# Stick-breaking sums as two rounded fp32r products instead of one f32 product

## Chip, core and metric

The kernel runs on one core of one Trainium2 chip. The metric is the device time of one execution in microseconds (us), as the median of several executions. The profile shown is of one more execution, taken by the hardware profiler.

## What is computed

Two blocks of a network, one after the other, on 512 tokens of width 1024. The change lies in the stick-breaking attention of the second block, which has 8 heads of width 128:

```
z = einsum('bhqd,bhkd->bhqk', q, k) * scale
causal = s_idx < t_idx
log_1mb = where(causal, log_sigmoid(-z), 0.0)
suffix = cumsum(log_1mb, axis=3, reverse=True) - log_1mb
log_a = log_sigmoid(z) + suffix
a = where(causal, exp(log_a), 0.0)
out = einsum('bhqk,bhkd->bhqd', a, v)
```

For a key s, `suffix` is the sum of the log terms of all later keys. In the kernel the keys lie on the 128 partitions, so that sum is a matrix product: with a triangle of ones inside a block of 128 keys, with a full matrix of ones over later blocks.

## The kernel before

All of the model is one program, written out by hand for each engine, with semaphores between them. The scores of a head are causal, so key block kb (0 to 3) only meets the query columns from 128*kb on: 512, 384, 256 and 128 columns. The four pieces of a head stand side by side in one tile of 1280 columns, at the offsets `offs` = 0, 512, 896, 1152. Three "parts" are worked on at a time, in the order m = 2, 1, 0: part 2 holds key blocks 2 and 3 (384 columns), part 1 key block 1 (384), part 0 key block 0 (512).

For each head h, in a pipeline over rounds:

- TensorE (PE), `sb_scores`: z of the head, an f32 product of 512, 384, 256 or 128 columns for each key block, to PSUM banks 4 to 6 (line L664).
- ScalarE (ACT): Abs (L970), Exp (L972), Ln (L974) of z, giving log(1+exp(-|z|)) in `sbt`; then, for the head before, the Exp that gives the weights a (L982), and the rounded copy `oH` of the output of two heads back (L977).
- VectorE (DVE), once the Ln is done (`sb_t`): for each part, `Lp` = max(z,0)+t, the negated log(1-beta) (L1170), then log beta in `sbt` (L1171), then the causal mask of the diagonal block (L1174, L1176). The last of these sends `sb_L`. I call these ten instructions the block of a head.
- PE, `sb_sums`: for each key block one f32 product of `Lp` with the triangle `low` (L672), and one with `ones` for every later key block (L675), summed in banks 0 to 2. In all ten f32 products a head: one of 512 columns, two of 384, three of 256, four of 128.
- DVE: subtracts the sums from log beta (L1190); ACT takes the Exp, DVE masks it (L1184), PE multiplies by v (L706), DVE takes the rest `oL` of the output (L1161).

PE's program is a fixed list. Round h holds, for kb = 3, 2, 1, 0 in turn, the scores of head h+1 and the sums of head h; then the product with v of head h-1; then `GATE_BLOCKS[h]` pieces of other work, (8, 8, 8, 5, 4, 4, 3, 4, 4) for the rounds 0 to 8. Such a piece is one eighth of a weight tile of the gate projection: three fp32r products of 512 columns (L1513 to L1515). After the rounds follow the tiles of `branch_sb` (operand `sb_oH`). The waits in the two functions are

```
E.at("sb_L", 3 * h - min(kb, 2))      # sb_scores(h, kb)
E.at("sb_L", 3 * h + 3 - min(kb, 2))  # sb_sums(h, kb)
```

so neither the scores of head h+1 nor the sums of head h start before the first `sb_L` of head h; key block 1 wants the second and key block 0 the third.

GpSimd (POOL) makes of every f32 weight tile in `sb_raw` a rounded part `wH` (L1496) and a rest `wL` (L1501). It has room for two rests, so each L1501 waits for PE to finish a tile. When a gate tile is complete, ACT copies it from bank 7 to `merged` (L1819) at places set by `GATE_COPIES = {0: 1, 1: 2, 2: 3, 3: 4, 5: 5, 7: 6, 9: 7}` (round of ACT: tile); the next gate tile uses the same bank and waits for that copy. Tile 5 is complete after the third gate piece of PE's round 4, and tile 6 with the last piece of round 6.

Of the kernel before, what the change touches and what calls it, by code (L numbers as in the profile page):

```python
# [19 lines left out]
P = 128  # L20
F32 = mybir.dt.float32
F32R = mybir.dt.float32r
# [7 lines left out]
S = 512  # L30
# [156 lines left out]
def build(nc, a, first=True, second=True):  # L187

    with ExitStack() as ctx:
# [7 lines left out]
        def sb(name, shape, dt=F32, on=None):  # L197
            return (on or ctx).enter_context(nc.sbuf_tensor("sb_" + name, shape, dt))
# [5 lines left out]
        par = sb("params", [P, N_KEPT])  # L204
        xT = sb("xT", [P, KB, S])
        hH = sb("hH", [P, KB, S], F32R)
# [14 lines left out]
        def C(name, i=0, n=None):  # L221
            o, w = CONSTS[name]
            return cst[:, o + i:o + i + (n or w)]
# [362 lines left out]
        def sb_in(first, kb):  # L586

            at = P * 2 if kb == TB - 1 else 0
            return ps[first + min(kb, 2)][:, at:at + qw[kb]]
# [3 lines left out]
                 (0, slice(offs[0], offs[1]), slice(0, qw[0]))]  # L593
        sb_t = [B["sbt"][:, c, :] for c in range(2)]
        V_BANK = (6, 2, 0, 1)
        sb_a = [b[:].rearrange("p s t -> p (s t)")[:, 0:1280] for b in (sq, tmp)]
# [15 lines left out]
        def second_pe(E, products, products_and_sums, parts_ready, one_tile, part_of_tile, rows_tile, turn, h_hi, h_lo):  # L612
# [56 lines left out]
            def sb_sums(h, kb):  # L669
                E.at("sb_L", 3 * h + 3 - min(kb, 2))  # L670
                E.at("sb_la", 3 * h - min(kb, 2))
                mm = nc.tensor.matmul(sb_in(0, kb), C("low"), B["Lp"][:, offs[kb]:offs[kb] + qw[kb]],  # L672
                                      start=True, stop=True)
                for later in range(kb + 1, TB):
                    mm = nc.tensor.matmul(sb_in(0, kb)[:, P * (later - kb):], ones,  # L675
                                          B["Lp"][:, offs[later]:offs[later] + qw[later]],
                                          start=False, stop=True, skip_group_check=True)
                if kb < TB - 1:
                    mm.then_inc(sems("sb_S"), 1)
# [251 lines left out]
        def second_act(E, eng, copy_tiles, squares_behind):  # L931
# [29 lines left out]
            E.meet()  # L961
            act.preload_act_table_set("natural_log_exp_and_others")
            copy_tiles("gate_sb", 1, lambda _: B["merged"][:, 0, :])
            for h in range(NH2 + 2):
                if h < NH2:
# [8 lines left out]
                    act.activation(t_all, t_all, ACT.Ln, bias=1.0).then_inc(sems("sb_t"), 1)  # L974
                if h >= 2:
                    E.wait("sb_o")
                    act.activation(B["oH"][:, h - 2, :], ps[3][:, :], ACT.Copy).then_inc(sems("sb_o_hi"), 1)  # L977
                if 1 <= h <= NH2:
                    for m, o, i in parts:
                        E.wait("sb_la")  # L980
                        E.at("sb_o", h - 2)
                        act.activation(sb_a[(h - 1) % 2][:, o], sb_t[(h - 1) % 2][:, o], ACT.Exp).then_inc(sems("sb_a"), 2 if m == 2 else 1)  # L982
                if h in GATE_COPIES:
                    copy_tiles("gate_sb", 1, lambda _: B["merged"][:, GATE_COPIES[h], :], at=GATE_COPIES[h])
# [163 lines left out]
        def second_dve(E, eng, chain, add_tiles):  # L1148
# [9 lines left out]
            def output_lo(h):  # L1158

                E.wait("sb_o_hi")  # L1160
                v.tensor_tensor(B["oL"][:, h, :], ps[3][:, :], B["oH"][:, h, :].bitcast(F32), ALU.subtract).then_inc(sems("sb_o_parts"), 1)  # L1161

            for h in range(NH2 + 1):
                if h < NH2:
                    E.wait("sb_t")
                    for m, o, i in parts:
# [8 lines left out]
                        d = slice(offs[m], offs[m] + P)  # L1175
                        v.tensor_tensor(B["Lp"][:, d], B["Lp"][:, d], C("ups"), ALU.mult).then_inc(sems("sb_L"), 1)  # L1176
                if h >= 2:
# [1185 lines left out]
```

## Time and profile before

| what | value |
|---|---|
| median of 3 executions | 3344.29 us (3342.53 to 3344.42) |
| the profiled execution | 3344.32 us, its span 3342.1 us |
| PE busy | 3247.6 us, 97% of the span |
| DVE busy | 2278.2 us, 68% |
| POOL busy | 1844.5 us, 55% |
| ACT busy | 750.3 us, 22% |

The span is what the profile's clock covers, from the first instruction to the last; 2.2 us of the execution's time lie around it. Times in the rows are counted from the start of the span. The rounds above take the stretch from about 990 to 1094 us.

### The profile page before, as it was taken

Reading aid. Unit: us, or ns where it says so; the run is one execution under the profiler, and the core shown is the slowest. Engines: PE = TensorE matmul, PEld = TensorE weight load, DVE = VectorE, ACT = ScalarE, POOL = GpSimd, SP = SyncE. Lnnn points to the kernel's source line nnn. Section 1 sums busy time; section 2 is a strip of 40 time slices with the busy share of each in tenths; the row PEclk is TensorE's granted clock in tenths of the full one; section 3 lists DMA queues with packets and bytes.
Section 4 is the critical chain, followed back from the end, with each engine's and each line's share of the span. In section 5 each row is a group of like instructions: output and inputs, shape, how many; then the busy total and the mean of one; then the engine's idle time right before and its main releaser. Section 6 shows DMA issues by size and latency. Waiting matters only on the chain.

```text
span 3342.1 us, 40578 instructions
## 1 busy us (share of the span) xinstructions
PE 3247.6 (97%) x15903; PEld 2695.6 (81%) x15903; DVE 2278.2 (68%) x3352; ACT 750.3 (22%) x1208; POOL 1844.5 (55%) x994
## 2 busy tenths in 40 slices
PE   6999999999999999999999999999999999999999
PEld 5777678887877887888888888888878887888887
DVE  6975389973426257776755888799963337888884
ACT  2142322211224221222121111255530011111110
POOL 4546367766542553011666666633356666777775
PEclk9999999999999999999999999999999999999999
DMA  3222122222320221000333444355553336566652
GB/s 133 82 64 95 45 95 95 96 99 90 107 76 32 82 85 61 14 15 31 120 105 117 139 139 139 133 184 210 186 183 123 123 120 197 188 200 195 199 194 99
DMA packets 164524, 391.67 MB, mean 117 GB/s; under 512 B 10864, under 2 KB 69488, under 8 KB 162288
## 3 DMA queue, kind: packets, MB, share of 16 engines
q1 hardware_dynamic: 73408, 262.70, 23.8%
q10 hardware_dynamic: 90928, 126.39, 11.1%
q8 instruction: 127, 2.08, 0.3%
q14 instruction: 61, 0.50, 0.0%
HBM read 326.14 MB, written 62.91 MB: 116 GB/s over the span
## 4 chain that ended last, share of the span: by engine, by line
PE 76%; DVE 19%; issue 2%; ACT 1%; DMA 1%; POOL 0%; ACTq 0%; DVEq 0%; POOLq 0%
PE banks L1513 21%; PE banks L1515 20%; PE banks L1514 20%; DVE sb_gated L1422 6%; DVE sb_sq L2192 3%; DVE sb_onehot L1419 2%; PE banks L378 1%; PE banks L792 1%; PE banks L804 1%; DVE sb_tmp L2202 1%; PE banks L801 1%; PE banks L1549 1%; DVE sb_sq L2190 1%; PE banks L1551 1%; PE banks L1550 1%
## 5 line engine op out<-in xcount | busy, mean ns | idle before, releaser
L1501 POOL TENSOR_TENSOR sb_wL<-sb_raw,sb_wH 128x1024 fp32r<-128x1024 f32 x495 | 1216.0, 2457 | 1471.1 <-PE banks L1515 1415.4
L1513 PE MATMUL banks<-sb_hH,sb_wH 128*128 128x512 f32 x2040 | 819.8, 402 | 13.2 <-ACT sb_sq L1117 3.7
L1515 PE MATMUL banks<-sb_hH,sb_wL 128*128 128x512 f32 x2040 | 796.9, 391 | 0.0
L1514 PE MATMUL banks<-sb_hL,sb_wH 128*128 128x512 f32 x2040 | 796.2, 390 | 0.0
L1496 POOL TENSOR_SCALAR sb_wH<-sb_raw 128x1024 fp32r<-128x1024 f32 x495 | 644.6, 1302 | 14.8 <-DMA sb_raw<-in_weights 14.8
L1513 PEld LDWEIGHTS banks<-sb_hH,sb_wH 128*128 128x128 f32 x2040 | 384.6, 189 | 97.2 <-issue 15.3
L1515 PEld LDWEIGHTS banks<-sb_hH,sb_wL 128*128 128x128 f32 x2040 | 383.5, 188 | 81.5
L1514 PEld LDWEIGHTS banks<-sb_hL,sb_wH 128*128 128x128 f32 x2040 | 384.5, 189 | 73.7 <-issue 1.9
L1513 PE MATMUL banks<-sb_pzH,sb_wH 128*128 128x512 f32 x1024 | 399.6, 390 | 5.9 <-DVE sb_xT L1465 3.8
L1514 PE MATMUL banks<-sb_pzL,sb_wH 128*128 128x512 f32 x1024 | 398.9, 390 | 0.0
L1515 PE MATMUL banks<-sb_pzH,sb_wL 128*128 128x512 f32 x1024 | 398.9, 390 | 0.0
L1513 PEld LDWEIGHTS banks<-sb_pzH,sb_wH 128*128 128x128 f32 x1024 | 192.6, 188 | 48.0 <-issue 4.2
L1422 DVE TENSOR_SCALAR sb_gated<-sb_consts,sb_slots 128x128 f32<-128x128 f32 x512 | 230.6, 516 | 0.0
L1456 DVE TENSOR_TENSOR sb_tmp<-sb_Ga,sb_Gt 128x512 f32<-128x512 f32 x96 | 222.7, 2320 | 7.8 <-DMA sb_Ga<-acts 7.8
L1515 PEld LDWEIGHTS banks<-sb_pzH,sb_wL 128*128 128x128 f32 x1024 | 192.5, 188 | 40.0
L1514 PEld LDWEIGHTS banks<-sb_pzL,sb_wH 128*128 128x128 f32 x1024 | 192.7, 188 | 39.8
L1095 ACT ACTIVATE sb_stage<-banks 128x512 f32<-128x512 f32 x128 | 144.9, 1132 | 142.6 <-PE banks L905 142.6
L1140 ACT ACTIVATE sb_pzH<-sb_tmp 128x512 fp32r<-128x512 f32 x96 | 60.6, 632 | 462.5 <-DVE sb_tmp L1456 462.5
L1465 DVE TENSOR_TENSOR sb_xT<-sb_xT,banks 128x512 f32<-128x512 f32 x104 | 71.5, 688 | 125.1 <-PE banks L1515 125.1
L1460 DVE TENSOR_TENSOR sb_pzL<-sb_tmp,sb_pzH 128x512 fp32r<-128x512 f32 x96 | 155.9, 1624 | 0.0
L905 PEld LDWEIGHTS banks<-sb_onehot,sb_gated 128*128 128x128 f32 x1024 | 132.0, 191 | 22.2 <-DVE sb_gated L1422 13.9
L2192 DVE SCALAR_TENSOR_TENSOR sb_sq<-sb_uab,sb_params,sb_sq 128x512 f32<-128x512 f32 x88 | 145.4, 1652 | 3.1
(429 smaller groups left out, 4688.5 us busy)
## 6 DMA issues: line engine op xcount, KB each, us to landing
sb_raw<-in_weights SPq DMA_DIRECT2D x495, 512.0 KB, 3.3
gates<-sb_stage ACTq DMA_DIRECT2D x16, 2048.0 KB, 7.8
acts<-sb_sq ACTq DMA_DIRECT2D x96, 256.0 KB, 2.0
sb_Gt<-gates ACTq DMA_DIRECT2D x24, 1024.0 KB, 7.1
sb_Ga<-acts ACTq DMA_DIRECT2D x24, 1024.0 KB, 10.7
sb_Gt<-gates ACTq DMA_DIRECT2D x4, 2048.0 KB, 10.3
sb_xT<-in_xT SPq DMA_DIRECT2D x4, 512.0 KB, 9.7
acts<-sb_xT ACTq DMA_DIRECT2D x1, 2048.0 KB, 7.8
```

Source lines behind the costliest of these rows:

```text
L905: mm = pe.matmul(ps[2 + r][:, x * P:(x + 1) * P], B["gated"][:, r, x], B["onehot"][:, r, x], start=True, stop=True)
L1095: act.activation(stage[:, :, 4 * r:4 * r + 4].rearrange("p e t -> p t e"), ps[2 + r % 4][:, :].rearrange("p (t e) -> p t e", t=4), ACT.Cop ...
L1422: ins = v.tensor_scalar(B["gated"][:, r % 4, x], C("iota"), at(1, x), at(2, x), ALU.is_equal, ALU.mult)
L1456: v.tensor_tensor(by_tg(tmp[:, e % 4, :]), by_tg(B["Ga"][:, e, :]), B["Gt"][:, :, e, :], ALU.mult).then_inc(sems("pz_v"), 1)
L1460: v.tensor_tensor(B["pzL"][:, (z + 1) % 2, e - 1, :], tmp[:, (e - 1) % 4, :], B["pzH"][:, (z + 1) % 2, e - 1, :].bitcast(F32), ALU.subtrac ...
L1465: empties(v.tensor_tensor(xT[:, e, :], xT[:, e, :], bank(t), ALU.add), t)
L1496: nc.gpsimd.tensor_scalar(wH[:, t % HIS, :], raw[:, t % RAWS, :], 1.0, 0.0, ALU.mult, ALU.add).then_inc(sems("weights_hi"), 1)
L1501: nc.gpsimd.tensor_tensor(wL[:, t % LOS, :], raw[:, t % RAWS, :], wH[:, t % HIS, :].bitcast(F32), ALU.subtract).then_inc(sems("weights_lo" ...
L1513: pe.matmul(out, hi, H, start=start, stop=False)
L1514: pe.matmul(out, hi, L, start=False, stop=False)
L1515: return pe.matmul(out, lo, H, start=False, stop=stop)
L2192: ins = v.scalar_tensor_tensor(out=to, in0=u[:, k:S + k], scalar=PM("ffn_w", wcol + k), in1=to, op0=ALU.mult, op1=ALU.add)
```

## The change

`Lp` is now also kept in two fp32r parts, rounded `Lp_hi` (a copy by ACT) and the rest `Lp_lo` (a subtraction by DVE). Every sum over more than 128 columns is done as two fp32r products instead of one f32 product, with `ones_r` or with a rounded triangle `low_r`. Sums over 128 columns stay f32. The new tiles lie where xT lies, which is not in use in this stretch (it was stored to memory before, semaphore `x_kept`); in the rows they are called `sb_parked_x`.

```
-        xT = sb("xT", [P, KB, S])
+        with ExitStack() as e:
+            xT = sb("xT", [P, KB, S], on=e)
+        parked = sb("parked_x", [P, KB * S], F32R)
...
+        Lp_hi, Lp_lo, low_r = parked[:, 0:1280], parked[:, 1280:2560], parked[:, 2560:2560 + P]
...  sb_sums
-                mm = nc.tensor.matmul(sb_in(0, kb), C("low"), B["Lp"][:, offs[kb]:offs[kb] + qw[kb]],
-                                      start=True, stop=True)
-                for later in range(kb + 1, TB):
-                    mm = nc.tensor.matmul(sb_in(0, kb)[:, P * (later - kb):], ones,
-                                          B["Lp"][:, offs[later]:offs[later] + qw[later]],
-                                          start=False, stop=True, skip_group_check=True)
+                for n in range(kb, TB):
+                    out, part = sb_in(0, kb)[:, P * (n - kb):], slice(offs[n], offs[n] + qw[n])
+                    exact = qw[n] > P
+                    if exact:
+                        mm = nc.tensor.matmul(out, ones_r[:] if n > kb else low_r, Lp_hi[:, part],
+                                              start=(n == kb), stop=True, skip_group_check=True)
+                        mm = nc.tensor.matmul(out, ones_r[:] if n > kb else low_r, Lp_lo[:, part],
+                                              start=False, stop=True, skip_group_check=True)
+                    else:
+                        mm = nc.tensor.matmul(out, ones if n > kb else C("low"), B["Lp"][:, part],
+                                              start=(n == kb), stop=True, skip_group_check=True)
...  ACT
+            eng.wait_ge(sems("x_kept"), 16)
...
-                if h >= 2:
-                    E.wait("sb_o")
-                    act.activation(B["oH"][:, h - 2, :], ps[3][:, :], ACT.Copy).then_inc(sems("sb_o_hi"), 1)
                 if 1 <= h <= NH2:
                     for m, o, i in parts:
                         E.wait("sb_la")
                         E.at("sb_o", h - 2)
                         act.activation(sb_a[(h - 1) % 2][:, o], sb_t[(h - 1) % 2][:, o], ACT.Exp).then_inc(sems("sb_a"), 2 if m == 2 else 1)
+                if h < NH2:
+                    for m, o, i in parts:
+                        E.wait("v_ready")
+                        act.activation(Lp_hi[:, o], B["Lp"][:, o], ACT.Copy).then_inc(sems("hi_ready"), 1)
+                if h >= 2:
+                    E.wait("sb_o")
+                    act.activation(B["oH"][:, h - 2, :], ps[3][:, :], ACT.Copy).then_inc(sems("sb_o_hi"), 1)
...  DVE
+            E.eng.wait_ge(sems("x_kept"), 16)
+            chain(v.tensor_copy(low_r, C("low")))
...
-                        v.tensor_tensor(B["Lp"][:, d], B["Lp"][:, d], C("ups"), ALU.mult).then_inc(sems("sb_L"), 1)
+                        v.tensor_tensor(B["Lp"][:, d], B["Lp"][:, d], C("ups"), ALU.mult).then_inc(sems("v_ready"), 1)
+                    for m, o, i in parts:
+                        E.wait("hi_ready")
+                        v.tensor_tensor(Lp_lo[:, o], B["Lp"][:, o], Lp_hi[:, o].bitcast(F32), ALU.subtract).then_inc(sems("sb_L"), 1)
```

On DVE, a round before: the ten instructions of the block, then the rest of an output, four masks and the three subtractions of the sums.

```order
L1170 SCALAR_TENSOR_TENSOR sb_Lp<-banks,sb_sbt 128x384
L1171 SCALAR_TENSOR_TENSOR sb_sbt<-banks,sb_sbt 128x384
L1176 TENSOR_TENSOR sb_Lp<-sb_Lp,sb_consts 128x128
L1170 SCALAR_TENSOR_TENSOR sb_Lp<-banks,sb_sbt 128x512
L1171 SCALAR_TENSOR_TENSOR sb_sbt<-banks,sb_sbt 128x512
L1176 TENSOR_TENSOR sb_Lp<-sb_Lp,sb_consts 128x128
L1161 TENSOR_TENSOR sb_oL<-banks,sb_oH 128x512
L1184 TENSOR_TENSOR sb_tmp<-sb_tmp,sb_consts 128x128 x4
```

The same place in the changed kernel, from part 1 of the block on (its lines L1185, L1186, L1191, L1174 and L1202 are the L1170, L1171, L1176, L1161 and L1184 of before).

```order
L1185 SCALAR_TENSOR_TENSOR sb_Lp<-banks,sb_sbt 128x384
L1186 SCALAR_TENSOR_TENSOR sb_sbt<-banks,sb_sbt 128x384
L1191 TENSOR_TENSOR sb_Lp<-sb_Lp,sb_consts 128x128
L1185 SCALAR_TENSOR_TENSOR sb_Lp<-banks,sb_sbt 128x512
L1186 SCALAR_TENSOR_TENSOR sb_sbt<-banks,sb_sbt 128x512
L1191 TENSOR_TENSOR sb_Lp<-sb_Lp,sb_consts 128x128
L1194 TENSOR_TENSOR sb_parked_x<-sb_Lp,sb_parked_x 128x384 x2
L1194 TENSOR_TENSOR sb_parked_x<-sb_Lp,sb_parked_x 128x512
L1174 TENSOR_TENSOR sb_oL<-banks,sb_oH 128x512
L1202 TENSOR_TENSOR sb_sq<-sb_sq,sb_consts 128x128 x4
```

`sb_L` moved from the three L1176 in the block to the three new L1194, which all stand behind the whole block.

On ACT, its round 5 before, from the Exp on, the one with the copy of gate tile 5:

```order
L972 ACTIVATE sb_sbt<-sb_sbt 128x1280
L974 ACTIVATE sb_sbt<-sb_sbt 128x1280
L977 ACTIVATE sb_oH<-banks 128x512
L982 ACTIVATE sb_sq<-sb_sbt 128x384 x2
L982 ACTIVATE sb_sq<-sb_sbt 128x512
L1819 ACTIVATE sb_merged<-banks 128x512
```

and in the changed kernel (L981, L983, L988, L995, L1837 are the L972, L974, L982, L977, L1819 of before; L992 is the new rounded copy of `Lp`):

```order
L981 ACTIVATE sb_sbt<-sb_sbt 128x1280
L983 ACTIVATE sb_sbt<-sb_sbt 128x1280
L988 ACTIVATE sb_sq<-sb_sbt 128x384 x2
L988 ACTIVATE sb_sq<-sb_sbt 128x512
L992 ACTIVATE sb_parked_x<-sb_Lp 128x384 x2
L992 ACTIVATE sb_parked_x<-sb_Lp 128x512
L995 ACTIVATE sb_oH<-banks 128x512
L1837 ACTIVATE sb_merged<-banks 128x512
```

The copy of the gate tile now stands behind the last rounded copy of `Lp` and the copy `oH`.

## Rows read from the trace of the kernel before

**Rows 1.** The page: the span, then busy time, share and instructions of each engine

```profile
span 3342.1 us, 40578 instructions
PE 3247.6 (97%) x15903; PEld 2695.6 (81%) x15903; DVE 2278.2 (68%) x3352; ACT 750.3 (22%) x1208; POOL 1844.5 (55%) x994
```

**Rows 2.** The chain that ended last, round 4: start, us, engine, what

```profile
1045.22 0.43 PE banks L672 x2
...
1046.53 0.65 PE banks L672 x2
...
1048.68 0.86 PE banks L672 x2
...
1055.09 0.61 ACT sb_merged L1819
```

**Rows 3.** Timeline of PE: first product of the rounds 0, 1, 3 to 7, and of `branch_sb`

```profile
990.48 0.38 PE L664 MATMUL banks<-sb_sbq,sb_sbk 128*128 128x128 f32 x2
...
1003.90 0.38 PE L664 MATMUL banks<-sb_sbq,sb_sbk 128*128 128x128 f32 x2
...
1032.12 0.38 PE L664 MATMUL banks<-sb_sbq,sb_sbk 128*128 128x128 f32 x2
...
1044.18 0.38 PE L664 MATMUL banks<-sb_sbq,sb_sbk 128*128 128x128 f32 x2
...
1056.60 0.38 PE L664 MATMUL banks<-sb_sbq,sb_sbk 128*128 128x128 f32 x2
...
1068.02 0.38 PE L664 MATMUL banks<-sb_sbq,sb_sbk 128*128 128x128 f32 x2
...
1078.72 0.82 PE L672 MATMUL banks<-sb_Lp,sb_consts 128*128 128x128 f32 x4
...
1093.68 0.39 PE L1513 MATMUL banks<-sb_oH,sb_wH 128*128 128x512 f32 x1
```

**Rows 4.** Timeline of PE: fp32r products of 256 columns, and one of 512

```profile
202.53 0.28 PE L1515 MATMUL banks<-sb_mH,sb_wL 128*128 128x256 f32 x1
202.64 0.28 PE L1513 MATMUL banks<-sb_mH,sb_wH 128*128 128x256 f32 x1
...
1031.89 0.39 PE L1515 MATMUL banks<-sb_hH,sb_wL 128*128 128x512 f32 x1
```

**Rows 5.** Timeline of round 3: DVE and ACT

```profile
1039.89 0.56 DVE L1170 SCALAR_TENSOR_TENSOR sb_Lp<-banks,sb_sbt 128x384 f32<-128x384 f32 x1 [0.32 <-ACT sb_sbt L974]
...
1041.46 1.45 ACT L982 ACTIVATE sb_tmp<-sb_sbt 128x384 f32<-128x384 f32 x3
...
1042.54 0.28 DVE L1176 TENSOR_TENSOR sb_Lp<-sb_Lp,sb_consts 128x128 f32<-128x128 f32 x1
...
1044.07 0.28 DVE L1176 TENSOR_TENSOR sb_Lp<-sb_Lp,sb_consts 128x128 f32<-128x128 f32 x1
...
1045.98 0.55 DVE L1190 TENSOR_TENSOR sb_sbt<-sb_sbt,banks 128x384 f32<-128x384 f32 x1 [0.22 <-PE banks L675]
```

**Rows 6.** Timelines of POOL, DVE and PE in round 0

```profile
990.80 2.36 POOL L1501 TENSOR_TENSOR sb_wL<-sb_raw,sb_wH 128x1024 fp32r<-128x1024 f32 x1 [4.27 <-PE banks L1515]
...
991.19 2.10 DVE L1176 TENSOR_TENSOR sb_Lp<-sb_Lp,sb_consts 128x128 f32<-128x128 f32 x1
...
993.35 0.91 PE L664 MATMUL banks<-sb_sbq,sb_sbk 128*128 128x384 f32 x2 [1.18 <-DVE sb_Lp L1176]
...
994.54 0.28 DVE L1176 TENSOR_TENSOR sb_Lp<-sb_Lp,sb_consts 128x128 f32<-128x128 f32 x1
```

**Rows 7.** PE behind two of its stalls, and a 1 us window with granted clock (PEclk)

```profile
2469.36 0.47 PE L1513 MATMUL banks<-sb_hH,sb_wH 128*128 128x512 f32 x1 [3.07 <-ACT sb_sq L1117]
...
2782.29 0.77 PE L1513 MATMUL banks<-sb_pzH,sb_wH 128*128 128x512 f32 x1 [3.78 <-DVE sb_xT L1465]
...
2785.37 0.40 PE L1514 MATMUL banks<-sb_pzL,sb_wH 128*128 128x512 f32 x1
...
2783.00:2784.00 1.00, 1.00 (x4) 0.81 (x3) 1.00 (x2) 0.63 (x1) 0.00 (x0) 0.50 1.13 317
```

## Prediction

> **What bounds the kernel now.** I read the page first: PE is busy for 97% of the span, every other engine for 68% or less [rows 1]. Saved PE work is saved time, then, as long as PE doesn't stand still in the place where it is saved. So I next laid out the changed stretch by its rounds, in the timeline of PE. Round 0 takes 13.42 us, rounds 1 and 2 together 28.22 (14.11 each), round 3 12.06, round 4 12.42, round 5 11.42, round 6 10.70, and rounds 7 and 8 together 14.96 [rows 3]. PE hardly waits in them: 1.18 us in round 0 [rows 6], about 0.8 in round 4 for the copy of gate tile 5 [rows 2], 0.6 in round 7. It is PE's work that sets the pace of each round before.
>
> Then I asked how much slack the others have. In round 3 (start 1032.12) DVE begins the block of head 4 at 1039.89, 7.77 us after the round's start, and ends it with the L1176 at 1044.07, 4.46 us later [rows 3, 5]. The first `sb_L` comes after the first quarter of that block, and PE needs it only at 1044.18. The chain scores, Abs, Exp, Ln, block has some 2 us to spare. The change spends on this slack.
>
> **What PE saves.** In the chain that ended last an f32 product takes 0.86, 0.65 and 0.43 us for 512, 384 and 256 columns [rows 2]. An fp32r product of 512 starts 0.23 us before the next (1031.89 to 1032.12), one of 256 0.12 [rows 3, 4]; 384 lies between, 0.17. Two passes against one: 0.86 - 0.46 = 0.40 once, 0.65 - 0.34 = 0.31 twice, 0.43 - 0.24 = 0.19 three times: 1.58 us per head, 12.6 in eight. For 384 the bounds are the neighbours' 0.12 and 0.23, which moves 1.58 by 0.2 either way.
>
> **What the chain gains in length.** PE now sends the last scores 0.68 us earlier in the round (the sums of key blocks 2 and 1 stand ahead of them: 0.19 + 0.31 + 0.19), so the block begins 7.09 us after the round's start. It still lasts 4.46. But `sb_L` now hangs on the new subtractions, and the first of them stands behind the whole block. No row has it; the nearest are a subtraction of 384 columns, 0.55 us [rows 5], and 0.28 for 128 columns in SBUF, so 0.3 to 0.7 bounds it; I take 0.5, near the row of the same width. Its rounded copy on ACT is hidden: three instructions of these sizes take 1.45 us together [rows 5], and part 2 is copied while DVE does part 0. From DVE's end to a restarted PE I count 0.17: L1176 ends at 993.29, PE starts at 993.35 and its first product takes 0.1 longer than the 0.65 above [rows 2, 6]. So no round with scores in it can be shorter than 7.09 + 4.46 + 0.50 + 0.17 = **12.2 us**. The wait is PE's first in the round, and behind it stand scores, sums, output and gate pieces, that is, everything.
>
> **What POOL adds.** In round 0 POOL's L1501 runs from 990.80 for 2.36 us, and the 128-column mask that DVE starts at 991.19 takes 2.10 us instead of 0.28 [rows 6]: 1.8 us lost. The Trainium skill (SBUF — State Buffer, "Who interferes with whom") says that a DVE instruction with two SBUF inputs and a GpSimd instruction that reads SBUF exclude each other for the whole instruction. By that rule, the trace agrees, the new subtractions can be held up too, and by the sum it doesn't matter which instruction of the block is hit. POOL starts 0.32 us after PE ends a gate tile (990.48 to 990.80) [rows 3, 6].
>
> **The sum, round by round** (own work of PE is the length before, less its waits, less 1.58):
> - Start of round 0: head 0's block ends at 994.82 [rows 6], then 0.50 + 0.17: 995.5 instead of 990.48. PE waits 5.0 us.
> - Round 0: own work 13.42 - 1.28 - 1.58 = 10.6, done at 1006.1; POOL from 1006.4 to 1008.8. DVE's block begins at 1002.6; its last mask is due 4.18 later, at 1006.8, and comes out at 1008.9. Round 1 starts at 1009.6, after a wait of 3.5.
> - Rounds 1, 2: own work 12.5, more than 12.2, so PE's work counts: 1022.1, 1034.7.
> - Round 3: own work 10.5, chain 12.2: 1046.9.
> - Round 4: the third gate piece ends at R + 9.1 = 1056.0 and fills tile 5. POOL runs from 1056.3 to 1058.7; DVE's mask of part 1, due 2.65 us into the block [rows 5] at 1056.6, loses 1.8. The block ends at 1060.3. ACT then still has the last rounded copy (0.65), `oH` (0.5) and the gate tile's copy (0.6 [rows 2]): 1062.0. Only then may the fourth piece start; it ends at 1062.9. PE waits 6.1 us in this round.
> - Round 5: 12.2: 1075.1.
> - Round 6: again three pieces, the same meeting with POOL: 12.2 + 1.8, so 1089.1, PE waits 4.9.
> - Rounds 7 and 8 have no scores: 14.96 - 0.6 - 1.58 = 12.8, so 1101.9.
>
> `branch_sb` started at 1093.68 before [rows 3]: **8.2 us later**. Behind it PE's list is as before, and I move it as a whole. The `x_kept` waits and the copy of the triangle cost nothing, since the store was long done and DVE stands idle ahead of head 0; without that cover the copy is one instruction, 0.3.
>
> **The clock.** Behind a stall of 3.78 us PE ran at granted clock 0.50, which is 1.2 instead of 2.4 GHz: the seven products from 2782.29 to 2785.37 took 3.08 us instead of 7 x 0.227 = 1.59, a loss of 1.5. Behind one of 3.07 us it did not (0.47 for the first product, not 0.77) [rows 7]. The three stalls of 4.9 us and more should each bring this, and the first two thirds of a round are on the chain, so it is not hidden: 3 x 1.5 = 4.5. The stall of 3.5 lies between the two rows; I leave it out. The Trainium skill (TensorE: Matmul & The Clock Gate, "What's actually happening") says that idleness throttles the array and activity releases it. By that page the sum is the one with 4.5, without it 8.2 alone.
>
> Together 8.2 + 4.5 = 12.7 us. The profiled execution took 3344.32, its span and 2.2 around it, and the median is 3344.29, so they serve alike: 3344.3 + 12.7 = **3357.0 us**.
>
> **The rivals.**
> 1. *Likeliest, 62%*: as above, 3353 to 3362. The upper end is 8.2 plus six lapses of the clock (also behind the stall of 3.5 and two of 2.4, 12.2 less the own work of rounds 5 and 4) at 1.5, 3361.5, and some for the new subtraction's upper bound (0.15 in five rounds).
> 2. *The chain as above, but the clock holds, 14%*: 3352.5. For it: the 3.07 us stall. Against: the 3.78.
> 3. *POOL and the masks miss each other, 12%*: in rounds 4 and 6 POOL starts only 0.3 us ahead of the mask. If DVE is first by that little, POOL waits instead, and the later mask loses 0.6 or less. That takes 1.2 off twice; with luck in round 0 as well (head 0's block ends at 993.0) and no lapse, the sum falls to about +0.7: 3345.0, within 0.2%.
> 4. *Faster, 5%*: the chain has slack after all, PE's work stays the bound, 12.6 us are saved: 3331.7. One mechanism would do it: a first `sb_L` that PE gets before it needs it. It decides at a chain of 9.1 us, round 6's own work; at 10.5 rounds 3 and 4 would already gain. The order of the instructions speaks against it, since the new subtraction can't pass the block.
> 5. *Worse still, 7%*: fp32r passes between f32 ones don't keep their 0.12 to 0.23. If they cost as much as the f32 product (0.86 for two of 512 would be no gain), rounds 1 and 2 lose their 3.2 and the end its 1.6: about 3362.
>
> I predict 3357.0, with a range of 3347 to 3363; it leaves out rival 4 and the luckiest part of 3. A measurement of this kernel tells 0.2%, 6.7 us, from nothing. Slower than 3351.0: cases 1, 2 and 5 and a little of 3, 0.80; within 0.2%: 0.14; faster: 0.06.
>
> **What would show it.** Right: PE waits for the new subtraction (L1194) at the head of rounds 0, 1, 3 or 4, 5, 6 and 7; rounds 3 and 5 at 12.2 us; one wait in round 4 for the copy of the gate tile; granted clock at 0.50 in the products behind the long ones; sums of a head 1.58 us shorter. Wrong: rounds 3 to 6 at 10.5, 9.9, 9.8 and 9.1 us, PE without waits, or a stretch behind `branch_sb` that is not the same length as before.

## The result, and the profile after

The changed kernel takes 3369.6 us (median of 4 runs, 3363.4 to 3377.4); beside it on the same chip the kernel before took 3344.4 (4 runs, 3342.5 to 3348.4). The ratio is 1.0073, with an interval of 1.0059 to 1.0088: slower by 25 us. I had predicted 3357.0 and a range of 3347 to 3363. The direction is right, the time lies outside the range.

The page of the changed kernel stands beside [rows 1]. PE's busy time is 0.8 us less than before, not 12.6: products at half clock count double. The span is 19.1 us longer.

```profile
span 3361.2 us, 40629 instructions
...
PE 3246.8 (97%) x15903; PEld 2700.3 (80%) x15903; DVE 2298.6 (68%) x3377; ACT 763.4 (23%) x1232; POOL 1845.4 (55%) x994
```

The list of PE's waits (engine and line, whom it waited for: us in total, times, the longest) names three that before had nothing of this size:

```profile
PE banks L667 <- DVE sb_parked_x L1194: 12.1, 4, 4.7
...
PE banks L1531 <- ACT sb_merged L1837: 5.9, 1, 5.9
...
PE banks L684 <- DVE sb_parked_x L1194: 4.7, 1, 4.7
```

That is 22.7 us of standing still: the new subtractions (L1194) at the heads of five rounds and the copy of gate tile 5 in round 4. The timeline of PE has the first product of head 0's scores, of rounds 0 to 6, of the late gate piece, of round 7 and of `branch_sb`. It answers to [rows 3]; the last bracket of a row is PE's idle time before it and who ended it.

```profile
981.61 2.32 PE L667 MATMUL banks<-sb_sbq,sb_sbk 128*128 128x128 f32 x8
...
994.11 0.80 PE L667 MATMUL banks<-sb_sbq,sb_sbk 128*128 128x128 f32 x2 [4.69 <-DVE sb_parked_x L1194]
...
1011.42 0.80 PE L667 MATMUL banks<-sb_sbq,sb_sbk 128*128 128x128 f32 x2 [4.01 <-DVE sb_parked_x L1194]
...
1026.59 0.38 PE L667 MATMUL banks<-sb_sbq,sb_sbk 128*128 128x128 f32 x2
...
1039.15 0.38 PE L667 MATMUL banks<-sb_sbq,sb_sbk 128*128 128x128 f32 x2
...
1051.20 0.49 PE L667 MATMUL banks<-sb_sbq,sb_sbk 128*128 128x128 f32 x2 [1.38 <-DVE sb_parked_x L1194]
...
1066.57 0.77 PE L1531 MATMUL banks<-sb_hH,sb_wH 128*128 128x512 f32 x1 [5.95 <-ACT sb_merged L1837]
...
1067.99 0.63 PE L667 MATMUL banks<-sb_sbq,sb_sbk 128*128 128x128 f32 x2
...
1081.66 0.80 PE L667 MATMUL banks<-sb_sbq,sb_sbk 128*128 128x128 f32 x2 [2.06 <-DVE sb_parked_x L1194]
...
1097.36 0.80 PE L684 MATMUL banks<-sb_Lp,sb_consts 128*128 128x128 f32 x2 [4.68 <-DVE sb_parked_x L1194]
...
1112.20 0.39 PE L1531 MATMUL banks<-sb_oH,sb_wH 128*128 128x512 f32 x1
```

From here on "the stage" is the stretch from the first scores of head 0 to `branch_sb`: 110.85 us before (982.83 to 1093.68), 130.59 now. The first scores in the timeline of before:

```profile
982.83 2.32 PE L664 MATMUL banks<-sb_sbq,sb_sbk 128*128 128x128 f32 x8
```

The difference of 19.7 us accounts for the span's 19.1. Set against the prediction, round by round:

| stretch | predicted | measured | more |
|---|---|---|---|
| first scores to round 0 | 12.7 | 12.50 | -0.2 |
| round 0 | 14.1 | 17.31 | 3.2 |
| round 1 | 12.5 | 15.17 | 2.7 |
| round 2 | 12.6 | 12.56 | 0.0 |
| round 3 | 12.2 | 12.05 | -0.1 |
| round 4 | 16.0 | 16.79 | 0.8 |
| round 5 | 12.2 | 13.67 | 1.5 |
| round 6 | 14.0 | 15.70 | 1.7 |
| rounds 7, 8 | 12.8 | 14.84 | 2.0 |
| sum | 119.1 | 130.59 | 11.5 |

Rounds 2 and 3 are as forecast within 0.15 us. All of the excess lies in rounds with or behind a stall, and nearly all of it in the first products behind the stall. In round 2 the last scores start 2.78 us after the round's start; in rounds 0, 1, 5 and 6 that takes 5.49, 5.41, 4.40 and 4.48. The windows of those places show why (columns: window, its length, PE busy and its instructions, granted clock, DMA share, GB/s):

```profile
990.00:995.00 5.00, 0.90 (x4) 0.78 0.31 105
995.00:1000.00 5.00, 5.00 (x17) 0.53 0.02 3
...
1010.00:1015.00 5.00, 3.58 (x13) 0.50 0.33 105
...
1065.00:1070.00 5.00, 3.43 (x11) 0.50 0.15 59
...
1080.00:1085.00 5.00, 3.34 (x11) 0.66 0.00 0
...
1095.00:1100.00 5.00, 2.64 (x11) 0.52 0.34 105
```

Five places at granted clock 0.50, 1.2 GHz; before, no window of the stage is below 1.00. I had forecast three lapses at 1.5 us. To compare them I use the clock's deficit: one less PEclk, times the window's length, added up over windows of 5 us. The five lapses have 3.45, 3.35, 3.4, 1.7 and 3.45. Outside the stage the deficit is nearly the same in both traces, 15.6 us before and 15.3 now, though not all in the same places, so on balance nothing was lost there.

The passes themselves are as cheap as forecast. In round 2, the last products of key block 1:

```profile
1028.75 0.33 PE L681 MATMUL banks<-sb_parked_x 128*128 128x384 f32 x1
1028.92 0.28 PE L679 MATMUL banks<-sb_parked_x,sb_ones_r 128*128 128x256 f32 x1
1029.04 0.27 PE L681 MATMUL banks<-sb_parked_x,sb_ones_r 128*128 128x256 f32 x1
1029.15 0.38 PE L684 MATMUL banks<-sb_Lp,sb_consts 128*128 128x128 f32 x2
```

Starts lie 0.17 us apart for 384 columns and 0.12 for 256, between f32 products. Round 2 is 12.56 against 14.11 before: 1.55 saved, 1.58 forecast.

### The profile page after: what moved, and what is told of

Same layout as the page of the kernel before. It is cut to its first block, busy times and chain, and to the rows that moved or that the text cites. A ratio compares the mean times of both kernels' runs of the same rounds, so it can differ in the third digit from the quotient of the medians.

```text
span 3361.2 us, 40629 instructions
## 1 busy us (share of the span) xinstructions
PE 3246.8 (97%) x15903; PEld 2700.3 (80%) x15903; DVE 2298.6 (68%) x3377; ACT 763.4 (23%) x1232; POOL 1845.4 (55%) x994
## 3 DMA queue, kind: packets, MB, share of 16 engines
q10 hardware_dynamic: 90928, 126.39, 11.1%
## 4 chain that ended last, share of the span: by engine, by line
PE 75%; DVE 19%; issue 2%; ACT 2%; DMA 1%; POOL 0%; ACTq 0%; DVEq 0%; POOLq 0%
PE banks L1531 20%; PE banks L1533 20%; PE banks L1532 20%; DVE sb_gated L1440 6%; DVE sb_sq L2210 3%; DVE sb_onehot L1437 2%; PE banks L380 1%; PE banks L800 1%; PE banks L812 1%; DVE sb_tmp L2220 1%; PE banks L809 1%; PE banks L1567 1%; DVE sb_sq L2208 1%; PE banks L1569 1%; PE banks L1568 1%
## 6 DMA issues: line engine op xcount, KB each, us to landing
sb_Ga<-acts ACTq DMA_DIRECT2D x24, 1024.0 KB, 11.1
```

## The experiments

The theory after this reading (A): chain and POOL cost what I had reckoned, and the clock took over twice its term. The rivals: the passes are what is slow (B); the products behind a stall are slow for another reason than the clock (D); POOL, or DVE's total work, sets the stage whatever the order (F).

### e1_products: the cheaper products without the chain

```diff
-chain(v.scalar_tensor_tensor(out=B["Lp"][:, o], ...))
+chain(v.scalar_tensor_tensor(out=Lp_hi[:, o], ...))
...
-    act.activation(Lp_hi[:, o], B["Lp"][:, o], ACT.Copy)
-    v.tensor_tensor(Lp_lo[:, o], B["Lp"][:, o], Lp_hi[:, o].bitcast(F32), ALU.subtract)
...
-    Lp_lo[:, part]
+    Lp_hi[:, part]
```

The masks work on `Lp_hi` too, and the last of each part gives `sb_L`.

> The products of the change alone: DVE writes the block of the log terms straight into the rounded tile, both fp32r passes read that tile, and `sb_L` comes from the block as before; ACT's rounded copies and DVE's subtractions are gone. The second pass therefore adds the rounded part again in place of the rest, and the narrow f32 product reads rounded values. Theory A (PE saves 1.58 us a head, the chain and the clock took more): no stall of PE at the heads of the rounds but for a meeting of POOL and a mask, rounds 3 to 6 at 10.5, 9.9, 9.8 and 9.1 us or up to 2 longer where POOL hits, 3331.7 to 3335, faster than before by about 10. Rival B (fp32r passes between f32 ones cost PE as much as the f32 product): 3344 or more. Rival C (the scores, Abs, Exp, Ln, block chain has less slack than I read): 3338 to 3342 with waits of PE for the block's last mask.

3337.9 us (7 runs, 3332.8 to 3343.8) beside 3348.1 for before: ratio 0.9973 (0.9959 to 0.9986). The stage takes 102.19 us, 8.7 less than before; rounds 2 and 3 take 12.55 and 10.51, as forecast. Rival B falls: the passes give back what they should. The median lies above the 3331.7 to 3335 that I expected, near rival C's price, but C falls too: PE doesn't wait in rounds 2 and 3, which are as short as PE's own work. Of the 3.9 us of the stage that are missing, 3.4 are lost from round 6 on. Three rows of its timelines, POOL's, DVE's and PE's:

```profile
1068.60 2.35 POOL L1512 TENSOR_TENSOR sb_wL<-sb_raw,sb_wH 128x1024 fp32r<-128x1024 f32 x1 [17.29 <-PE banks L1526]
...
1068.86 2.23 DVE L1187 TENSOR_TENSOR sb_parked_x<-sb_parked_x,sb_consts 128x128 fp32r<-128x128 f32 x1
...
1071.14 0.44 PE L679 MATMUL banks<-sb_parked_x 128*128 128x384 f32 x1 [2.02 <-DVE sb_parked_x L1187]
```

Faster rounds brought the end of a gate tile, and with it POOL's subtraction, onto DVE's mask: 2.23 us instead of 0.28, a stall of 2.02, and granted clock 0.50 behind it (deficit 1.7).

### e2_chain: the chain without the cheaper products

```diff
-                    exact = qw[n] > P
+                    exact = False
```

> The chain of the change alone: ACT's rounded copies, DVE's subtractions and the late `sb_L` stay, but every sum is the f32 product of before and the split is not used. Theory A (the chain and its stalls are the loss, the saved PE work only lightens it): 12 to 14 us above before without the clock, and 8 to 12 more from lapses behind the stalls, since the waits at the heads of the rounds stay longer than 2 us in rounds 0, 1 and 7 and in round 4's gate piece: about 3366, 3358 to 3372; the first sums of a head 1.58 us longer than in the changed kernel. Rival B (the fp32r passes are dear, above all behind an idle PE, and are what the clock term really was): products of before are back, so 3352 to 3357, and no long stretch at granted clock 0.50.

3366.5 us (4 runs) beside 3348.1: ratio 1.0069 (1.0049 to 1.0089). The stage takes 131.64 us, 20.8 more than before, with three lapses (deficits 3.4, 1.7 and 1.7) behind stalls of 4.69, 4.43 and 4.01 us. There are no fp32r sums in it, and the lapses are there all the same: B falls a second time. That the whole change is no faster than its chain alone is the point of the case. Where PE waits for the chain, cheaper products only make the wait longer (4.01 instead of 0.62 at the head of round 1, 1.38 instead of 0.52 at that of round 4); some 6 of the 12.6 us go that way. The rest is real, but the clock takes it: five lapses in the changed kernel against three here. Without what the clock costs behind the stalls (6.0 us here, 11.8 in the changed kernel, estimates from the granted clock behind each stall, as shown under e8) the stages would be 125.6 and 118.8 us.

### e3_fill: no stall for the clock to see

```diff
+            def fill(n):
+                for _ in range(n):
+                    nc.tensor.matmul(ps[1][:, 384:512], ones, ident, start=True, stop=True, skip_group_check=True)
...
+            FILL, FILL_COPY = {0: 19, 1: 14, 4: 5, 6: 8, 7: 20}, 25
...
+                    if (b, k) == (6, 0):
+                        E.at("sb_la", 15)
+                        fill(FILL_COPY)
...
             for h in range(NH2 + 1):
+                if h in FILL:
+                    E.at("sb_la", 3 * h)
+                    fill(FILL[h])
```

> The changed kernel, with products of 128 f32 columns (ones by the identity) into the unused last quarter of bank 1, where PE would stand still: 19 at the start of round 0, 14 of round 1, 8 of round 6, 20 of round 7 and 25 ahead of the gate piece of round 4 that waits for the copy. Nobody reads them. Theory A (five lapses of the clock behind stalls cost about 11.6 us beyond the chain): granted clock 1.0 in the products behind these places, each round's last scores 2.8 us after the round's start instead of 4.4 to 5.5, and 3352 to 3356, so 8 to 12 above before. Rival D (the products behind a stall are slow for another reason: fp32r passes or operands late in SBUF): the offsets stay at 4.4 and more and the time at 3363 to 3377, or higher by what the extra products overrun.

3355.4 us (8 runs) beside 3348.1: ratio 1.0027 (1.0011 to 1.0043). The stage takes 119.49 us, 8.6 more than before; the forecast without the clock was 8.2. Round 0, with the 19 fillers (38 records) ahead of it, and a window:

```profile
996.37 4.40 PE L692 MATMUL banks<-sb_consts 128*128 128x128 f32 x38
...
1001.24 0.49 PE L667 MATMUL banks<-sb_sbq,sb_sbk 128*128 128x128 f32 x2 [0.46 <-DVE sb_parked_x L1206]
...
1004.12 1.02 PE L667 MATMUL banks<-sb_sbq,sb_sbk 128*128 128x512 f32 x2
```

```profile
1000.00:1010.00 10.00, 9.54 (x52) 1.00 0.15 52
```

The last scores come 2.88 us after the start, where they took 5.49. The same chain, the same waits, but PE busy in them: 11.1 us of the stage come back, nearly all of the 11.5 that my sum had missed. D falls.

### e4_early: the gate tile's copy ahead of the split

```diff
+                if h == 5:
+                    copy_tiles("gate_sb", 1, lambda _: B["merged"][:, GATE_COPIES[h], :], at=GATE_COPIES[h])
                 if h < NH2:
                     for m, o, i in parts:
                         E.wait("v_ready")
...
-                if h in GATE_COPIES:
+                if h in GATE_COPIES and h != 5:
```

> The changed kernel with ACT's copy of gate tile 5 moved ahead of the three rounded copies in its round, so that PE can start the fourth gate piece of round 4 while ACT is still at work on the split. Theory A: PE's stall of 5.9 us in round 4 shrinks to 3.5 or less, the lapse behind it gets shorter or goes, and round 5 starts up to 2 us earlier: 2 to 4 us below the changed kernel, 3360 to 3368. Rival E (the stall's end is set by POOL and DVE's masks and not by ACT's order): no change of round 4, 3363 to 3377. The spread of the changed kernel's own times, 14 us, makes the rows of round 4 the better witness than the median.

3371.3 us (4 runs) beside 3348.1: ratio 1.0080 (1.0060 to 1.0100), no gain. The trace says where it went. The stall of 5.95 became two, of 0.78 and 3.00, and round 5 starts 83.75 us after the first scores, where it was 86.38: 2.6 earlier. But the lapse behind the 3.00 now falls wholly into round 5, whose last scores come at 5.50 instead of 4.40; at the head of round 7 more of the lapse lies behind the stall than in the changed kernel (a deficit of 2.9 against 2.4, which costs, as e8 will show); and at `branch_sb` only 0.6 is left (stage 129.97). E falls, and my expectation that the lapse would shrink with the stall falls too.

### e8_dose_up and e9_dose_down: what a stall costs

The kernel before, with PE's scores waiting for the whole block of the head before:

```diff
-                E.at("sb_L", 3 * h - min(kb, 2))
-                E.at("sb_ls", 3 * h - min(kb, 2))
+                E.at("sb_L", 3 * h)
+                E.at("sb_ls", 3 * h)
...
+                        for _ in range(REPEATS.get(h, 0) if m == 0 else 0):
+                            chain(v.tensor_tensor(B["Lp"][:, d], B["Lp"][:, d], C("ups"), ALU.mult))
```

> The kernel before, with PE's scores waiting for the whole block of the head before, and DVE repeating the last mask of heads 2 to 6 (11, 13, 8, 11 and 11 times, each 0.28 us) so that PE stands still at the heads of rounds 2 to 6 for about 1.5, 2.0, 2.5, 3.0 and 4.0 us; values don't change. It asks what stall brings granted clock 0.50 and what that costs, read from the distance of the round's last scores (3.48 us after its start at full clock). If a lapse hangs on the length of the one stall, as I predicted (3.07 us none, 3.78 us one, 1.5 each): distances of 3.5 to 3.6 up to 3.0 us and 5.0 behind 4.0. If shorter stalls bring it and it costs more, as the changed kernel's trace suggests: 5 or more from 2.0 us on. Some 18 to 26 above before in all.

> As e8_dose_up with the stalls the other way round: the last mask of heads 2 to 6 repeated 20, 17, 8, 7 and 2 times, stalls of about 4.0, 3.0, 2.5, 2.0 and 1.5 us at the heads of rounds 2 to 6. If the length of the one stall decides, each length does what it did in the other kernel. If it also depends on what PE did before, or on where the stall falls, a length of 2 to 3 us lapses in one kernel and not in the other.

One execution of each: 3393.3 and 3386.5 us. The stalls came out longer than I had aimed at. For the longest POOL is the reason, which met the repeated masks: 20 of them took 9.31 us ahead of the stall of 7.33 in e9, 11 took 6.33 ahead of that of 4.39 in e8, where one is 0.28. Three pairs of rows of PE's timeline (a round's first product and its last scores; 3.48 us apart at full clock), two of e8 and then one of e9:

```profile
1031.32 0.80 PE L664 MATMUL banks<-sb_sbq,sb_sbk 128*128 128x128 f32 x2 [4.39 <-DVE sb_Lp L1179]
...
1037.74 1.02 PE L664 MATMUL banks<-sb_sbq,sb_sbk 128*128 128x512 f32 x2
...
1070.54 0.49 PE L664 MATMUL banks<-sb_sbq,sb_sbk 128*128 128x128 f32 x2 [2.64 <-DVE sb_Lp L1179]
...
1075.81 1.02 PE L664 MATMUL banks<-sb_sbq,sb_sbk 128*128 128x512 f32 x2
```

```profile
1102.18 0.49 PE L664 MATMUL banks<-sb_sbq,sb_sbk 128*128 128x128 f32 x2 [1.36 <-DVE sb_Lp L1179]
...
1105.76 1.02 PE L664 MATMUL banks<-sb_sbq,sb_sbk 128*128 128x512 f32 x2
```

All of them, by length of stall:

| stall (us) | 0.16 | 1.36 | 2.63 | 2.64 | 4.00 | 4.22 | 4.22 | 4.29 | 4.39 | 5.04 | 5.31 | 6.35 | 7.33 |
|---|---|---|---|---|---|---|---|---|---|---|---|---|---|
| last scores later by | 0.1 | 0.1 | 1.8 | 1.8 | 1.6 | 2.8 | 2.8 | 1.8 | 2.9 | 2.1 | 2.5 | 2.4 | 1.5 |
| clock deficit | 0 | 0 | 1.7 | 1.7 | 1.7 | 3.4 | 3.4 | 1.7 | 3.4 | 3.4 | 3.4 | 3.3 | 3.4 |

A lapse costs the path 1.5 to 2.9 us, on average 2.2, and its deficit is about 1.7 or 3.4, in nothing between. The length of the stall doesn't set the price: 7.33 us cost 1.5, 4.39 cost 2.9. My 1.5 was the lowest of these prices, from a single row.

What sets the price can be read from the same traces. Half clock can begin before the stall ends, and that part of it costs nothing. Here are the windows of the stall and of the time behind it, for the stall of 7.33 us (e9) and for that of 4.39 (e8):

```profile
1022.53:1029.86 7.33, 0.00 (x1) 0.73 0.22 72
1029.86:1035.00 5.14, 5.14 (x19) 0.72 0.01 3
```

```profile
1026.93:1031.32 4.39, 0.00 (x1) 0.89 0.20 55
1031.32:1040.00 8.68, 8.68 (x24) 0.66 0.09 34
```

In e9 2.0 us of the deficit lie in the stall and 1.4 behind it, in e8 0.5 and 3.0. The delays were 1.5 and 2.9: the price is the deficit behind the end of the stall. That holds for each of the 11 lapses within 0.1 us.

### after_again: the changed kernel once more

> The changed kernel once more, unchanged, beside the others on this chip: its distance to before again 19 to 29 us, and a second trace for the lapses. If they hang on the stalls, the same five places show granted clock 0.50 and the offsets of the last scores are 4.4 to 5.5 again, within a few tenths of those of the first trace or with other values between 1.4 and 3 more than 2.8.

3365.3 us (4 runs, 3362.2 to 3377.2) beside 3346.0: ratio 1.0070 (1.0046 to 1.0095). The stage takes 129.55 us. Four of the five lapses are there again, with the same stalls to 0.01 us. The fifth is not, behind the same stall of 2.06; two rows and the window:

```profile
1081.19 0.49 PE L667 MATMUL banks<-sb_sbq,sb_sbk 128*128 128x128 f32 x2 [2.06 <-DVE sb_parked_x L1194]
...
1084.08 1.02 PE L667 MATMUL banks<-sb_sbq,sb_sbk 128*128 128x512 f32 x2
```

```profile
1080.00:1085.00 5.00, 3.81 (x21) 1.00 0.01 3
```

2.89 us to the last scores, against 4.48. Two executions of one program differ in whether a stall of 2 us brings a lapse.

### e5_inter: the subtractions between the parts of the block

```diff
-                    for m, o, i in parts:
...
+                    block(*parts[0])
+                    block(*parts[1])
+                    rest(*parts[0])
+                    log_beta(*parts[0])
+                    block(*parts[2])
+                    rest(*parts[1])
+                    log_beta(*parts[1])
+                    rest(*parts[2])
+                    log_beta(*parts[2])
```

`block` is the maximum-and-add with its masks, `log_beta` the minimum-and-subtract (`sb_ls`), `rest` the new subtraction (`sb_L`).

> The changed kernel with DVE's block reordered so that each part's subtraction follows as soon as its rounded copy is there, and the gate tile's copy early as in e4; PE's order as in the changed kernel. Theory A: the first `sb_L` comes about 2 us earlier and the chain no longer stands in the way in rounds 2 to 6, but the `sb_ls` of the last part comes later, and POOL can still hit: `branch_sb` 1 to 3 us earlier than before, 3341 to 3346, within 0.2% of before. Rival F (DVE's total work in the block, not its order, is the bound): rounds 3 to 6 near 12 us again, 3352 or more.

3353.5 us (9 runs) beside 3347.7: ratio 1.0016 (1.0002 to 1.0029). The stage takes 112.37 us, 1.5 more than before where I expected 1 to 3 less. Rounds 2 and 3 are free of the chain (12.56 and 10.51), against F, though the time is one that F had named. But `sb_ls` of every part now comes behind a subtraction, and PE's scores wait for it instead: 2.10 and 2.31 us in rounds 0 and 1, 1.83 at the head of round 5. POOL has its part in each of the three, for it met that subtraction (1.38, 2.71 and 1.85 us where 0.55 is usual). The one in round 1:

```profile
1010.67 2.71 DVE L1202 TENSOR_TENSOR sb_parked_x<-sb_Lp,sb_parked_x 128x384 fp32r<-128x384 f32 x1
```

The stage has two lapses, behind the 1.83 and behind a stall of 2.79 in round 7. Better than the change, no better than before.

### e7_scores_first: the scores ahead of the sums

```diff
 def sb_scores(h, kb):
-                E.at("sb_L", 3 * h - min(kb, 2))
                 E.at("sb_ls", 3 * h - min(kb, 2))
...
                     if h + 1 < NH2:
                         sb_scores(h + 1, kb)
+                for kb in reversed(range(TB)):
                     if h < NH2:
                         sb_sums(h, kb)
```

> The changed kernel with the round reordered on PE: the four scores of the next head stand ahead of all sums of this one, and they wait only for DVE's last read of their bank (`sb_ls`), no longer for `sb_L`; the gate tile's copy of e4 is kept. Theory A (the loss is a chain of dependent steps, not the work): the last scores start about 1.3 us after the round's start instead of 2.8 to 5.5, the new subtractions run beside the scores, rounds 1 to 6 fall back to PE's own work (12.5, 12.5, 10.5, 10.7, 9.8 us and round 6 within 3 of 9.1), and `branch_sb` starts 5 to 8 us earlier than before: 3336 to 3340 where before stands at 3344. Rival F (POOL's meetings with DVE and the end at round 7 set the stage, whatever PE's order): no better than before, 3344 to 3352. Rival G (the log terms' rest is still late for the first sums): stalls behind the scores of 2 us and more in each round, 3350 and above.

3344.5 us (12 runs) beside 3347.7: ratio 0.9994 (0.9984 to 1.0004). It undoes the loss, 25 us, with the whole split in place, but 3336 to 3340 it isn't. The stage takes 107.07 us, 3.8 less than before where I expected 5 to 8; rounds 2, 3 and 4 take 12.56, 10.52 and 10.87. Left are a stall of 2.45 inside round 0 (no lapse) and one of 4.00 at the head of round 7 (deficit 1.7), both behind a mask that met POOL (2.12 and 2.00 us for 0.28). In part F was right: POOL's meetings are what is left, once the chain is gone.

### e10_first_fill: e7 with fillers

11 of e3's fillers ahead of the last scores of round 0, and 17 ahead of the sums of round 7.

> The kernel of e7, with products that nobody reads (128 f32 columns, ones by the identity, into the unused quarter of bank 1) in the two places where its trace shows PE standing still and the clock falling behind it: 11 ahead of the last scores of round 0 (stall 2.45 us) and 17 ahead of the sums of round 7 (stall 4.00). Theory A (a lapse costs 1.5 to 2.9 us behind any stall of 2 us and more, as in the two dose kernels): the stage from the first scores to `branch_sb` shrinks from 107.1 to some 103 us, about 4 below e7 and 7 below before. Rival (the lapses of e7 cost nothing, being hidden by the chain behind them): the stage stays at 107.

3347.4 us (10 runs) beside 3346.0: ratio 1.0001 (0.9990 to 1.0012). The stage takes 105.56 us, 1.5 less than e7 where I expected 4: round 0 is as long as in e7 (13.39 and 13.38), since its stall had brought no lapse, and the stretch from round 6 to `branch_sb` went from 27.53 to 26.04. One lapse, 1.5 us. I had read a stall of over 2 us as a lapse without looking at its window.

### e11_first_pool and e12_before_pool: POOL held back

```diff
+        POOL_AFTER = {1: (3, 0), 2: (6, 4), 3: (9, 8), 4: (12, 12), 5: (18, 20), 6: (24, 28)}
...
                     pool.wait_ge(sems("tile_done"), t - LOS + 1)
+                    done = t - LOS - TILE["gate_sb"] if "gate_sb" in TILE else 0
+                    if done in POOL_AFTER:
+                        pool.wait_ge(sems("sb_L"), POOL_AFTER[done][0])
+                        if POOL_AFTER[done][1]:
+                            pool.wait_ge(sems("sb_am"), POOL_AFTER[done][1])
                 nc.gpsimd.tensor_tensor(wL[:, t % LOS, :], ...)
```

> The kernel of e7, with POOL's subtraction of the weights (`wL`) held back in this stage until DVE has done the block, the split and the masks of the head at hand, so that the two don't meet. Nothing is filled in. Theory A with POOL as the second cause (each meeting costs DVE about 1.8 to 2 us and brings PE's stall over 2 us, so that a lapse comes on top): PE's stalls in rounds 0 and 7 fall from 2.45 and 4.00 to 1.5 us and less, no granted clock of 0.50 in the stage, the stage 98 to 100 us against 107.1 of e7 and 110.9 of before: 3331 to 3336 where before stands at 3344, faster by 0.2 to 0.4%. Rival (the held back POOL is late for PE's next gate tile, or its instruction meets DVE elsewhere): new waits of PE for POOL, and no better than e7.

> The kernel before with POOL held back as in e11 and nothing else: the control for it. PE's own work bounds the rounds there, so only the stall of 1.18 us in round 0 and a part of that of round 7 can go: 0 to 1.7 us below before, no difference that can be measured. If it is faster by 5 or more, e11's gain is POOL's and not the order of the scores.

e11 takes 3339.7 us (11 runs, 3332.0 to 3346.2) beside 3346.0: ratio 0.9978 (0.9967 to 0.9989). Its stage takes 99.02 us, 11.8 less than before. PE waits about as long in it as before, so of the 12.6 us that the split saves PE nearly all arrive. In the median only 6.3 us arrive, and it lies above the 3331 to 3336 that I expected; the profiled execution took 3335.3. POOL's and DVE's rows in round 0 are apart, the wait at the head of round 7 is down to 1.45, and no window of the stage is below 1.00. Its timelines of DVE, POOL and PE, and one window:

```profile
994.28 1.62 DVE L1196 TENSOR_TENSOR sb_parked_x<-sb_Lp,sb_parked_x 128x384 fp32r<-128x384 f32 x3
...
996.08 2.40 POOL L1528 TENSOR_TENSOR sb_wL<-sb_raw,sb_wH 128x1024 fp32r<-128x1024 f32 x1 [8.17 <-DVE sb_parked_x L1196]
...
1070.55 0.49 PE L683 MATMUL banks<-sb_Lp,sb_consts 128*128 128x128 f32 x2 [1.45 <-DVE sb_parked_x L1196]
```

```profile
1060.00:1075.00 15.00, 13.55 (x70) 1.00 0.01 2
```

e12 takes 3352.9 us (10 runs) beside 3346.0: ratio 1.0017 (1.0003 to 1.0030), against my expectation of no difference. Its stage is 108.59, 2.3 less than before, so the control says what it should of e11: POOL alone is worth 2.3, and with it held back in both kernels the split with the scores first is worth another 9.6 us of the stage. Between the stage and the median lie 9 us. The profiled execution has a deficit of 10 us 460 us behind the stage, which the last section tells of.

## Why the prediction was wrong

**The chain** (12.2 us for a round with scores): right. Round 3 took 12.05 and round 4's head waited 1.38. Among the signs I had also named a wait at the head of round 5; my own sum has none there, and the trace neither.

**The saved products** (1.58 a head): right, 1.55 in round 2, and alone they make the kernel faster (e1).

**POOL's meetings**: right in place and size, masks of 2.12, 1.95 and 2.23 us for 0.28 in the blocks of heads 0, 1 and 5, and a fourth meeting in the block of head 7. Held back, with the scores first, they are gone (e7 against e11: 8.1 us of the stage, lapses included).

**The sum without the clock** (8.2): right, 8.6 in e3, where no round is off its forecast by more than 0.6 us, so the agreement isn't one of errors that cancel. **The copy of gate tile 5** (PE waits 6.1 us): right, 5.95.

**The clock** is the step that failed: "The three stalls of 4.9 us and more should each bring this, and the first two thirds of a round are on the chain, so it is not hidden: 3 x 1.5 = 4.5. The stall of 3.5 lies between the two rows; I leave it out." There were five lapses in place of three. The stall left out (4.01) had one, and so had one of 2.06. And each cost more than 1.5: by the later last scores 2.7, 2.6, 2.3 (0.7 in the gate piece and 1.6 in round 5) and 1.7, in round 7 about 2.0. Together that is 11.3 us for a term that I had put at 4.5, and e3 gives back 11.1. Another 0.5 us in round 0 is POOL's: the three new subtractions took 2.45 us instead of 1.62 beside its rounding of the next tile, an instruction that my sum had left out (timeline of POOL):

```profile
1009.88 1.08 POOL L1514 TENSOR_SCALAR sb_wH<-sb_raw 128x1024 fp32r<-128x1024 f32 x1
```

The other terms came out 0.3 shorter, which leaves the 11.5 of the table.

Both errors have one origin: I took the threshold and the price from two rows. The 1.5 was as cheap as the cheapest lapse of the dose kernels. It belongs to a deficit of 1.7, 0.2 of it still in the stall of 3.78; the same trace of before has two lapses of 3.4 (160 to 170 and 1305 to 1315), a size that my term didn't allow for. The deficits behind the ends of the five stalls add up to 11.8 us, so the price found in e8 and e9 fits here too. And the stall of 3.07 us without a lapse [rows 7] was chance. All 13 other traces have the same wait, of 3.06 to 3.35 us, and in 11 of them half clock sets in around its end; only in e2 (3.17) and e12 (3.09) it doesn't. The shortest, in e8, and a window behind it:

```profile
2517.19 0.47 PE L1516 MATMUL banks<-sb_hH,sb_wH 128*128 128x512 f32 x1 [3.06 <-ACT sb_sq L1117]
```

```profile
2518.60:2521.90 3.30, 3.30 (x9) 0.50 0.97 243
```

The upper end of my range did count six lapses, but again at 1.5 each; at 2.2 it would have been 3366.

With 11.5 in place of 4.5 the sum is 3364.0, and the profiled execution took 3363.4. The median lies 6 us higher, 3369.6. Over the four runs the time goes with the mean granted clock, 0.991 for 3363.4 and 0.987 for 3377.4. That points to the clock for the rest as well, but it isn't shown: where it fell in the runs without a trace isn't known.

Rival 5 (dear passes) would have come nearer to the time, 3362, for a reason that the traces exclude. Rival 2 (the clock holds) is e3 with its fillers, 7.3 us above before. Rival 4 (faster) had its decision right: with a chain that doesn't hold PE up the split is a gain, and e11, with POOL held back besides, is that kernel.

## What to carry to other kernels

A cheaper instruction on the busiest engine pays only if what it waits for keeps pace. Before splitting an operand, walk the loop from the last product of one round to the first of the next, and look for work that needs none of the new results and can stand in front of them: here the next head's scores, held up only by a semaphore that said more than they needed. In this kernel a stall of PE of 3.8 us and more cost its length plus the half clock that was left behind its end, 1.5 to 3.0 us; one between 1.8 and 3.4 us may or may not bring a lapse, and a forecast should carry both cases.

## What the hardware showed

- A stall of PE brings granted clock 0.50 behind it or not. In the stage, up to 1.45 us none did (1.36, 1.38 and 1.45). In between it goes both ways: 1.83 and 2.79 (e5), 2.02 (e1), 2.63 (e9), 2.64 (e8) and 3.00 (e4) did, 2.10 and 2.31 (e5) and 2.45 (e7) did not, and at 2.06 the same program did in one execution and not in the next. Behind the stage a wait of 3.06 to 3.35 did in 11 of 14 traces. From 3.78 up all did. The deficit is 1.7 or 3.4 us. The length of a stall isn't all that decides: outside the stage the clock fell in before at 829.47, 4 us behind a wait of 1.12 us, and in the changed kernel the same wait (1.13) brought nothing.
- The half clock can also hold while PE is fully busy. Windows of PE in e12 at 1550 to 1565, and under them one of before at the same work:

```profile
1550.00:1555.00 5.00, 3.84 (x21) 1.00 0.01 3
1555.00:1560.00 5.00, 5.00 (x23) 0.53 0.00 0
1560.00:1565.00 5.00, 5.00 (x16) 0.50 0.00 0
```

```profile
1560.00:1565.00 5.00, 5.00 (x33) 1.00 0.00 0
```

PE's work there is a group of 8 products with a single column each (L378) after every six wide ones. With e12 the clock fell at the second of the eight groups, after a wait of 0.90 us ahead of the first, and came back at the seventh: a deficit of 10 us. In before the same wait stands ahead of them and the clock stayed at 1.00. The traces of e1, e3, e5, e7, e8, e9 and e10 have the long one as well (6.8 to 8.6), those of before, of the changed kernel (both), e2, e4 and e11 not. The runs of before without a trace have mean clocks from 0.992 to 0.997, so some of them may have something of this size too. It would explain why comparisons of whole kernels here spread over 10 us and more, while the stage of the changed kernel, traced twice, repeated to 1.1 us, and why e10, e11 and e12 are slower than their stages say; for the runs without a trace that isn't shown. What decides it stays open; no experiment was made on it.
